# Attention over compressed blocks, moved from a stage of its own into the quarters of the compression before it

## What is computed

```python
kc = rms_norm(compress(k_cmp, cmp_pos[0], cmp_w1[0], cmp_b1[0], cmp_w2[0]), kn_cmp)
vc = compress(v_cmp, cmp_pos[1], cmp_w1[1], cmp_b1[1], cmp_w2[1])   # gelu(flat @ w1 + b1) @ w2
s = jnp.einsum('btgnd,bcgd->btgnc', qg, kc) * scale
p_cmp = masked_softmax(s, c_mask[None, :, None, None, :])
o_cmp = jnp.einsum('btgnc,bcgd->btgnd', p_cmp.astype(vc.dtype), vc)
imp = jnp.sum(imp.reshape(B, Tq, NSA_KV_HEADS, n_sel, SLC_BLOCK // CMP_STRIDE), axis=-1)
_, sel = lax.top_k(imp, n_top)          # blocks for the selected-block branch
```

## Time and profile before

| | us |
|---|---|
| median of 3 runs | 2151.06 |
| lowest, highest | 2149.54, 2152.37 |
| the profiled execution | 2149.72 |
| its span, first to last instruction | 2147.9 |
| TensorE busy | 1971.1 |
| VectorE busy | 1139.9 |
| ScalarE busy | 830.7 |
| GpSimd busy | 689.0 |
| compression, layer 0 | 353.3 to 503.2 |
| attention over compressed blocks, layer 0 | 503.5 to 535.6 |
| samples' branches, layer 0 | 535.6 to 612 |

### The profile page before, as it was taken

The page is one execution under the profiler, slowest core; times in us unless marked ns, Lnnn a source line. Parts: engine busy times, 40 slices in busy tenths (PEclk is TensorE's granted clock), DMA queues, the critical chain, the costliest instruction groups (busy, mean ns, idle before and its releaser), DMA issues. The chain is left out here.

```text
span 2147.9 us, 38078 instructions
## 1 busy us (share of the span) xinstructions
PE 1971.1 (92%) x15341; PEld 1837.8 (86%) x15341; DVE 1139.9 (53%) x1929; ACT 830.7 (39%) x1813; POOL 689.0 (32%) x470
## 2 busy tenths in 40 slices
PE   7999799886889999999999987997968899999998
PEld 6999557886679999999989974687956899999998
DVE  3688754335344555455538876542353545555554
ACT  4593354432434222323147823643323431313130
POOL 2345344320023433333323652433100333333431
PEclk9999899996989999999999997998969899999999
DMA  4321421203522223222222132132063222222221
GB/s 150 97 63 38 143 62 54 71 21 118 157 59 80 79 79 96 82 79 79 79 81 80 61 112 72 41 88 57 1 192 83 79 79 81 94 82 79 79 82 62
DMA packets 200637, 175.77 MB, mean 82 GB/s; under 512 B 11356, under 2 KB 198030, under 8 KB 200334
## 3 DMA queue, kind: packets, MB, share of 16 engines
q1 hardware_dynamic: 196994, 170.16, 26.0%
q10 hardware_dynamic: 3468, 3.17, 0.5%
HBM read 162.67 MB, written 10.62 MB: 81 GB/s over the span
## 5 line engine op out<-in xcount | busy, mean ns | idle before, releaser
L427 POOL TENSOR_TENSOR WX<-RAW,WX 128x2048 fp32r<-128x2048 f32 (+2 forms) x48 | 222.6, 4638 | 622.0 <-ACT WX L423 622.0
L2337 DVE TENSOR_TENSOR sq<-sq 128x288 f32<-128x288 f32 x128 | 157.1, 1232 | 196.6 <-ACT sq L2306 196.6
L427 POOL TENSOR_TENSOR m_wl<-RAW,m_wh 128x2048 fp32r<-128x2048 f32 x36 | 166.5, 4625 | 284.9 <-ACT m_wh L423 284.9
L439 PE MATMUL bank<-UH,m_wl 128*128 128x288 f32 x640 | 188.6, 295 | 0.0
L438 PE MATMUL bank<-UL,m_wh 128*128 128x288 f32 x640 | 188.5, 295 | 0.0
L437 PE MATMUL bank<-UH,m_wh 128*128 128x288 f32 x640 | 188.4, 294 | 0.0
L439 PE MATMUL bank<-UH,WX 128*128 128x288 f32 x576 | 169.8, 295 | 0.0
L438 PE MATMUL bank<-UL,WX 128*128 128x288 f32 x576 | 169.6, 294 | 0.0
L437 PE MATMUL bank<-UH,WX 128*128 128x288 f32 x576 | 169.5, 294 | 0.0
L423 ACT ACTIVATE WX<-RAW 128x2048 fp32r<-128x2048 f32 (+1 forms) x48 | 92.0, 1916 | 173.9 <-PE bank L439 150.8
L1546 PE MATMUL bank<-FTS,W1S 128*128 128x256 f32 (+1 forms) x512 | 159.2, 311 | 0.0
(11 more groups left out here) (388 smaller groups left out, 5926.9 us busy)
## 6 DMA issues: line engine op xcount, KB each, us to landing
RAW<-in_w_up SPq DMA_DIRECT2D x32, 1024.0 KB, 5.4
RAW<-in_w_down SPq DMA_DIRECT2D x32, 1024.0 KB, 5.0
RAW<-in_w_in SPq DMA_DIRECT2D x20, 1024.0 KB, 5.2
R<-in_cache_nsa_kv SPq DMA_DIRECT2D x128, 64.0 KB
HT<-in_cache_nsa_kv SPq DMA_DIRECT2D x128, 64.0 KB, 2.6
RAW<-in_w_in SPq DMA_DIRECT2D x6, 1056.0 KB, 5.2
R2s<-in_cache_nsa_kv SPq DMA_DIRECT2D x48, 128.0 KB, 3.9
out<-R SPq DMA_DIRECT2D x10, 512.0 KB, 5.6
```

The lines of the kernel that those rows point to most:

```text
L427: eng.tensor_tensor(S.granule(S.wl, i, w)[:, chunks], S.granule(S.raw, i, w)[:, chunks], S.granule(S.wh, i, w)[:, chunks].bitcast(F32), AL ...
L439: ins = pe.matmul(out, wl[:, c, cols], ah[:, c, n], start=False, stop=(c == KC - 1))
L2337: dve.tensor_tensor(relu[n % 4], relu[n % 4], relu[n % 4], ALU.mult).then_inc(sem("relu_squared"), 1)
```

## The change

The stage "attention over compressed blocks" is dissolved. Its steps become functions that the loops over the quarters call at fixed g on each engine. Where they stand:

| | TensorE | ScalarE | VectorE |
|---|---|---|---|
| clear, spread queries, spread keys | | | 3, 5, 8 |
| prompt's scores (two tiles each) | 9, 11 | | |
| shift, exponentials, probabilities | | 11, 15 | 10, 14; 12, 13, 16, 17 |
| turn probabilities | 15, 18 | 16, 19 | |
| gates, samples' scores, softmax | 21 | 22 | 18, 22, 23 |
| sums, turned probabilities, block left out | 24 | 25 | 25 |
| prompt's values, branch added | 24, 26, 26, 28 | | 25, 27, 27, 29 |

Only `ssT` by `VC` and the gate remain, at the start of the samples' block; the first `scores` waits for them (`oa_made`). To make room in PSUM, turning uses two banks instead of three, and narrow units share one bank for both halves. `outputs(w)` moves from q = 3 to q = 2, `key_sums`, `key_factors`, `keep_keys`, `norm_keys` and `keep_values` move by about a quarter. GpSimd copies the entries of quarter g + 1 in its step g, ahead of the subtraction. SP loads samples 1, 0, 2 and 3, in this order, from within the compression; ScalarE issues no loads any more. The bodies of the moved functions are as before, but for banks and tiles. The diff, cut:

```diff
+            csT = [cut(2 * 2 * P), RAW[:, 3072:3072 + 4 * P]]
+            KD = cut(NKV * NCP)
+            cm = [cut(24) for _ in range(NT)]
+            imp, val = (cut(NP_ * 16).rearrange("p (a j) -> p a j", a=NP_) for _ in range(2))
+            QD = [QT[:, k, 0:SEQ].rearrange("p (b r) -> p b r", b=NB) for k in range(2)]
+            sBD = QT[:, 2, 0:SEQ].rearrange("p (a c) -> p a c", a=NP_)
+            ssT = QT[:, 3, 0:SEQ].rearrange("p (a r) -> p a r", a=NP_)
+            cs = [KT[:, t // 2, t % 2 * 256:t % 2 * 256 + 256] for t in range(NT)]
...
+            slots = [(HT_, 0, HT_, 2048), (RAW, 0, RAW, 2048), (R1, R_HG, R1, R_HI + SLOT), (R1, R_HI + 1024, R1, R_HI + 3072)]
...
+            def load_past(sp, b):
+                page = page_numbers(mybir.EngineType.SP, NPG * b)
+                for j in range(NPG):
+                    sp.dma_start(past_of(b)[:, j, :], cache_nsa_kv[bass.ds(l, 1), bass.ds(page[j], 1), :, 2:4].rearrange(
...
             def turn_bank(e):
-                return bank[4 + e % 3]
+                return bank[4 + e % 2]
...
-                n = chunks_of(w)
-                return bank[2 * (w % 2) + h][:, 0:NKV * n].rearrange("p (v n) -> p v n", v=NKV)
+                n = NKV * chunks_of(w)
+                p = CU[w][1]
+                return bank[h][:, 0:n] if p == 0 else bank[2 + (p - 1) % 2][:, h * n:(h + 1) * n]
...
+                return bank[6 if t % 2 else 1]
...
+                    sp.wait_ge(sem("w1_v_lo"), 4)
+                    load_past(sp, 1)
+                    sp.wait_ge(sem("raw_apart"), RAW_DONE[7])
+                    load_past(sp, 0)
+                    sp.wait_ge(sem("raw_apart"), RAW_DONE[9])
+                    sp.wait_ge(sem("c_scored"), 2)
+                    sp.wait_ge(sem("qd_made"), 1)
+                    load_past(sp, 2)
+                    load_past(sp, 3)
...
+                    for e in entries(0):
+                        rows_apart(e)
                     for g in range(NCQ):
-                        for e in entries(g):
+                        for e in entries(g + 1) if g + 1 < NCQ else ():
                             rows_apart(e)
...
@@ -1519,8 +1588,8 @@
                     def turn(e):
                         r = 2 * NEXT if TE[e][2] else P
                         pe.wait_ge(sem("raw_apart"), e + 1)
-                        if e >= 3:
-                            pe.wait_ge(sem("ct_lo"), e - 2)
+                        if e >= 2:
+                            pe.wait_ge(sem("ct_lo"), e - 1)
...
+                    def prompt_scores(i):
+                        pe.wait_ge(sem("kd_made"), 1)
+                        if i:
+                            pe.wait_ge(sem("c_shifted"), 2)
...
+                        for t in (2 * i, 2 * i + 1):
+                            for g in range(NG):
+                                o = t % 2 * 256 + g * NKV * NCP
+                                ins = pe.matmul(bank[6][:, o:o + NKV * NCP], QN[:, g, t * P:(t + 1) * P], KD, start=True, stop=True)
+                        ins.then_inc(sem("c_scored"), 1)
...
+                    def prompt_turn(i):
+                        pe.wait_ge(sem("c_shifted"), NT)
+                        pe.wait_ge(sem("c_probs"), 2 * i + 2)
+                        if i:
+                            pe.wait_ge(sem("c_turn_kept"), 1)
...
+                        ins.then_inc(sem("c_turned"), 1)
...
+                    def sample_scores():
+                        pe.wait_ge(sem("qd_made"), 1)
+                        pe.wait_ge(sem("kc_normed"), 4)
+                        pe.wait_ge(sem("c_turn_kept"), 2)
+                        pe.wait_ge(sem("gate_masked"), 1)
...
+                                  start=True, stop=True).then_inc(sem("s_scored"), 1)
...
+                    def sample_turn():
+                        pe.wait_ge(sem("s_probs"), 1)
+                        pe.matmul(bank[6][:, 0:NP_ * NCS], const("groupsum"), sp_, start=True, stop=True).then_inc(sem("s_imp"), 1)
+                        pe.wait_ge(sem("cx_kept"), 5)
+                        pe.wait_ge(sem("s_apart"), 1)
...
+                        ins.then_inc(sem("s_turned"), 1)
...
+                    def prompt_values(t):
+                        if t == 0:
+                            pe.wait_ge(sem("vc_kept"), 1)
+                            pe.wait_ge(sem("cx_kept"), 5)
+                        pe.wait_ge(sem("c_turn_kept"), t // 2 + 1)
+                        if t == 1:
+                            pe.wait_ge(sem("imp_made"), 1)
+                        elif t:
+                            pe.wait_ge(sem("c_kept"), t - 1)
...
+                        ins.then_inc(sem("c_valued"), 1)
...
                     for g in range(NCQ):
                         for e in entries(g):
                             turn(e)
+                        if g == 0:
+                            pe.wait_ge(sem("ft_cleared"), 1)
                         hidden(g)
                         w, q = g // 4 - 1, g % 4
-                        if q == 3 and w >= 0:
+                        if q == 2 and w >= 0:
                             outputs(w)
-                        if q == 0 and w >= 1 and CU[w - 1][0] == 0:
-                            key_sums(w - 1)
+                        if q == 3 and w >= 0 and CU[w][0] == 0:
+                            key_sums(w)
+                        if g in (9, 11):
+                            prompt_scores((g - 9) // 2)
+                        if g in (15, 18):
+                            prompt_turn((g - 15) // 3)
+                        if g == 21:
+                            sample_scores()
+                        if g == 24:
+                            sample_turn()
+                            prompt_values(0)
+                        if g == 26:
+                            prompt_values(1)
+                            prompt_values(2)
+                        if g == 28:
+                            prompt_values(3)
                     outputs(len(CU) - 1)
...
+                    def exponentials(t):
+                        act.wait_ge(sem("c_shifted"), t + 1)
+                        act.activation(cs[t], cs[t], ACT.Exp).then_inc(sem("c_exp"), 1)
+                    def keep_prompt_turn(i):
+                        act.wait_ge(sem("c_turned"), i + 1)
+                        if i:
+                            act.wait_ge(sem("w1_v_lo"), 4)
+                        act.activation(csT[i], bank[6][:, :], ACT.Copy).then_inc(sem("c_turn_kept"), 1)
...
+                    for g in range(NCQ + 2):
                         for e in entries(g) if 0 < g < NCQ else ():
                             keep_hi(e)
                         w, q = g // 4 - 1, g % 4
-                        if q == 0 and w >= 1 and CU[w - 1][0] == 0:
-                            keep_keys(w - 1)
                         if 13 <= g < 17:
                             split_weights_hi(act, 1, g - 13)
                         if q == 0 and w >= 0:
                             gelu_x(w)
+                        if q == 0 and w >= 1 and CU[w - 1][0] == 0:
+                            key_factors(w - 1)
                         if q == 1 and w >= 0:
                             gelu_sigmoid(w)
-                        if q == 1 and w >= 1 and CU[w - 1][0] == 0:
-                            key_factors(w - 1)
+                        if q == 3 and w >= 0 and CU[w][0] == 0:
+                            keep_keys(w)
+                        if g in (11, 15):
+                            for t in (0, 1):
+                                exponentials((g - 11) // 2 + t)
+                        if g in (16, 19):
+                            keep_prompt_turn((g - 16) // 3)
+                        if g == 22:
+                            act.wait_ge(sem("s_shifted"), 1)
+                            act.activation(sp3[:, :, 0:NC], sp3[:, :, 0:NC], ACT.Exp).then_inc(sem("s_exp"), 1)
+                        if g == 25:
+                            act.wait_ge(sem("s_turned"), 1)
+                            act.activation(ssT, bank[0].rearrange("p (a r) -> p a r", a=NP_), ACT.Copy)
...
-                @block.sync
-                def _(sp):
-                    for b in (0, 2, 3):
-                        load_past(sp, b)
...
-                    pe.wait_ge(sem("qd_made"), 2)
...
-                        ins = pe.matmul(bank[6][:, a * P:(a + 1) * P], ssT[:, a, :], VC[:, a, :], start=True, stop=True)
-                    ins.then_inc(sem("s_valued"), 1)
-                    prompt_values(0)
-                    for t in range(1, NT):
-                        prompt_turn(t)
-                        prompt_values(t)
...
+                    def clear_zeros():
+                        for x in (QD[0], QD[1], sBD, DMk, KD):
+                            dve.memset(x, 0.0)
+                        step(dve, dve.memset(VB, 0.0), "dve_done")
+                    def spread_queries():
```

(67 more changed lines are left out.)

335 lines of the change are left out of this document (110 added, 225 removed).

## The result

The changed kernel takes 2101.59 us (median of 4 runs, 2100.33 to 2104.12) against 2151.72 us (4 runs, 2149.54 to 2152.68): a ratio of 0.977, 95% interval 0.9753 to 0.9787. The forecast was 2093 us in a range of 2074 to 2120. The gain is 50.1 us where 58.4 were worked out; the span went from 2147.9 to 2098.4 us, 49.5 us less.

What follows compares the result with a forecast made beforehand. TensorE was taken as the bound, except in the serial attention stage and the stalled quarters 13 to 20. Terms summed to -29.2 us per layer, -58.4 for both: from 2149.7 us plus 1.3 to 2093 us, range 2074 to 2120.

Steps and rivals of the forecast that it cites:

- Term 1: The stage "attention over compressed blocks" disappears, apart from a 0.3 us handover: -31.8 us per layer.
- Term 2: The stage's TensorE work moves into the compression and counts in full, near the full clock: +11.0 us per layer.
- Term 3: Quarters 13 to 20: GpSimd copying a quarter ahead removes stalls, less new waits of 2.4, 1.0, 2.2 us: -10.8 us per layer.
- term 6: VectorE's 24.0 us moved into the compression, and the moved loads, costed at nothing.
- D: Quarters 13 to 20: the switch's excess nearly vanishes, -17 us instead of -10.8; 2081 us; chance 0.06.
- rival C: Near the switch of weights, GpSimd's subtraction blocks VectorE steps: 3.8 us per layer more, 2101 us; chance 0.12.
- Term 4: Compression's start and elsewhere: with two turning banks, turns wait for low parts: +2.0 us per layer, bounds 0 to 4.
- the tail stays: Compression's end: the 4.95 us wait for the last gelu and its 1.94 us of outputs stay unchanged.
- Term 5: Start of the samples' block: ssT by VC and VectorE's multiplications before `oa_made`: +0.4 us per layer, 0 to 2.9.
- A: Switch of weights: GpSimd's copies did not hold it, so moving them gains 0; 2114 us; chance 0.14.
- B: Compression: VectorE's and ScalarE's in-order queues bind, +14 us per layer; 2121 us; sign: compression over 165 us; chance 0.12.
- E: Two turning banks make every quarter wait for low parts: +16 us per layer, slower at 2183 us; chance 0.04.

Runs made afterwards that it cites:

- the last experiment: shift(2) moved to quarter 12 and shift(3) to 13, instead of both at 14, on top of the kernel of five moves: 2079.32 us, ratio 0.9663.
- the first alone: First two probabilities both in step 11 instead of steps 12 and 13, on the changed kernel: 2095.75 us, ratio 0.9746.
- the kernel of five moves: Changed kernel with probabilities at 11, outputs(2) and outputs(3) a quarter later, prompt's entry turned second, prompt_turn(0) at 16, outputs(6) behind the last quarter: 2091.2 us.

## Why the prediction was right, and where its sizes were off

**Term 1** (-31.8): the last output's end to the first turn of the samples' keys is 0.65 us, where 503.15 to 535.60 were 32.45. Right.

**Term 2** (+11.0): by its groups the new TensorE work is 11.8 us in layer 0, with records that overlap; it ran at the full clock, as taken.

```profile
L1665 PE MATMUL bank<-R 128*128 128x64 f32 x32 | 3.8, 272 | 0.0
...
L1713 PE MATMUL bank<-R 128*64 128x128 f32 x32 | 2.2, 279 | 0.0
L1713 PE MATMUL bank<-RAW,R 128*64 128x128 f32 x32 | 2.1, 276 | 0.0
...
L1676 PE MATMUL bank<-cst,R 128*128 128x128 f32 x8 | 1.3, 280 | 0.0
```

The 32 records (16 products) that took 7.1 us in the stage take 3.8 us. Right.

**Term 3 and term 6** hold the largest part of the miss. Term 3 left quarters 13 to 20 at 47.5 - 10.8 = 36.7 us; with the 1.3 us of prompt turns, which term 2 has, that is 38.0. They take 40.8 and 41.6 us, so term 3 is -8.0 us in layer 0 and not -10.8. Its three waits came at their places and sizes: 2.28 us (said 2.4), 1.01 (1.0), 2.12 (2.2). GpSimd ahead alone is worth 15.6 us; term 3 without these three waits is 16.4, so that part was sized well, and D's -17 was the alternative with no new waits at all. What was sized too small is what stood beside the waits. The work without stalls was put at 28.1 us, and the last experiment shows TensorE busy 29.84 us in it at the full clock. The clock behind the waits and collisions had 3 us together and took some 5.6 (40.84 - 29.84 - 5.41). In that lies the wait of 1.96 us at the second turn of quarter 14, and in layer 1 also the 1.98 us at prompt_turn(0). Neither was in the list, and both follow from VectorE instructions that GpSimd holds. The step that missed them is the sixth, "costed at nothing: VectorE's 24.0 us". It argued with VectorE's share (60%) and with the distance in quarters; but several of the moved operations have two SBUF inputs, and some of these stood where GpSimd subtracts. With all six moves the stretch is 31.6 us, 9.2 us less. Of that 6.5 us come with the last move; the first alone, which also only takes VectorE's instructions out of a subtraction, gave 5.8 us in both layers together.

That is **rival C's** mechanism, and about at its price: C had 3.8 us a layer, and the waits of TensorE that follow from collisions are 1.96 us in layer 0 and 3.94 us in layer 1, without what they cost in clock. That the measured 2101.6 us is also C's 2101 is in part luck: of the 5.3 us by which the sum of layer 0 misses, only 2.8 are in term 3 (below). C had a chance of 0.12 and should have had more: the mechanism was already in rows 5 and 7, and only the places were open. The Trainium skill ("SBUF — State Buffer", Who interferes with whom) says that a VectorE instruction with two SBUF inputs contends with a GpSimd one that reads SBUF, and that one with at most one SBUF input, outside VectorE's two-port modes, does not; the rows of the last experiment agree on both sides, 1.44 us against 0.41 and 0.42.

**Term 4** (+2.0): quarter 1 is turned at 365.86. That is 3.4 us later than before, of which 0.77 us come from the block ahead, whose last products start at 350.24 instead of 349.47; the rest is 2.7 us. Two banks alone cost 1.4 to 4.7 us a layer. Right within its bounds.

**A term that was missing:** outputs(6) stood behind the last quarter, inside the wait for the last gelu, and the change moved it to the quarter before. Its 0.84 us had cost nothing and now cost their length: the wait for the last gelu is 5.79 us in layer 0 and 6.06 us in layer 1, where it was 4.95 in both. The prediction said "the tail stays".

**Term 5** (+0.4): from the first turn of keys to the last wait of the samples' block it is 73.08 us, 71.93 before: 1.15. The trade that the term describes came out: the products of ssT by VC take 1.15 us to the next instruction, the wait of 0.79 us for ScalarE's keys is gone, and the first scores don't wait for `oa_made`; that is 0.36 us. The other 0.8 us are clock. The first 24 records of turning keys take 5.14 us at a granted clock of 0.50, directly behind the wait for the last gelu and its outputs; before they took 4.34 us at 0.64. No term had that.

The sum for layer 0, counted from the start of the last products ahead of the compression: -31.8 + 11.2 - 8.0 + 2.7 + 0.84 + 1.15 = -23.9 us, where the forecast was -29.2. The 11.2 is what is left over for term 2, with the 1.3 us of prompt turns in it (its records gave 11.8), so that the sum closes by itself. The miss of 5.3 us is 2.8 in term 3, 0.8 in the keys' slow turns, 0.8 in outputs(6), 0.7 in term 4 and 0.2 in term 2. Twice 23.9 is 1.7 us less than the 49.5 us of the span. From the samples' block of layer 0 (607.53 before, 584.42 after) to the last products ahead of layer 1's compression (1407.50, 1381.80), where the diff changes nothing, the changed kernel's profile is 2.6 us shorter, and ahead of layer 0's compression it is 0.77 us longer. That is scatter, and not the change.

**Rivals A, B and E** did not come: the copies were the holder (15.5 us back without them), the compression took 157.8 us and not 165 (but more than the 152 said), and no narrow quarter outside the switch waits. The loads were hidden, as said, and cost 33.5 us in both layers together if they are not moved along.

## What to carry to other kernels

When work is moved under other work, look at what each of its instructions reads and at what runs on the neighbouring engine at that moment, and not only at the engines' shares: two VectorE operations with both inputs in SBUF, put beside GpSimd's subtractions, held TensorE up by 3.64 us; away from there the stretch was 6.5 us a layer shorter. When a removed wait comes back at the next instruction, stop moving the waiters and look for an instruction on the releasing engine that takes longer than its own usual time. And before a stage is dissolved, list what lay hidden in its waits: here loads worth 33 us in both layers and an output of 0.84 us in each.

## What was not expected of the hardware

A VectorE operation that GpSimd holds can be passed over more than once. In the kernel of five moves L1942 started at 424.63, under a copy. Three GpSimd instructions that started after it went first: a copy at 424.69, the subtraction at 425.06 and a copy at 427.34 (0.39 us). L1942 ended at 428.01, 0.28 us after the last of them: 3.38 us for 0.42 us of work, more than the length of one subtraction (2.33).

Whether it is passed over was not the same each time. In the changed kernel the second shift's L1937 starts 0.28 us after the first of two GpSimd copies, in both layers. In layer 0, at 428.06, it took 0.43 us, and the second copy took 0.62 us. In layer 1 it took the 3.06 us shown above, through the second copy and the subtraction behind it, and the two copies kept their usual length:

```profile
1459.02 0.74 POOL L1572 COPY R<-HT 128x256 f32<-128x256 f32 x2
```

In the kernels with only the probabilities moved or only outputs(6) moved it took 3.05 or 3.06 us in both layers, and prompt_turn(0) waited 1.97 to 1.99 us. So layer 0 of the changed kernel is the exception among these six layers, and nothing in the profile tells why.

The clock after a wait did not always fall. The changed kernel has the same two waits, 1.96 and 2.28 us, in front of the same instructions in both layers. Its stretches behind them (columns as in the earlier trace rows), layer 0 and layer 1:

```profile
425.93:430.25 4.32, 4.32 (x30) 4.32 (x29) 3.09 (x5) 2.49 (x6) 4.32 (x6) 0.75 0.05 14
1456.70:1461.60 4.90, 3.73 (x32) 3.54 (x30) 4.80 (x5) 2.18 (x5) 4.90 (x6) 1.00 0.04 11
```

In layer 0 the granted clock is 0.75, and the eight records (four products) of outputs(2) took 1.12 us, the level of 1.2 GHz; in layer 1 it is 1.00, and they took 0.66 us. The faster layer 1 came out no shorter, 41.61 us against 40.84, since it has the 1.98 us in front of prompt_turn(0). A wait's price in clock could not be read off its length here. After the longer wait of 3.64 us, in the kernel of five moves, both layers ran slow: 0.59 of the full clock over 7.26 us in layer 0 and 0.74 over 5.96 us in layer 1.
